# Redistributing the retrieval rows over the attention units of a hybrid streaming encoder step

## The chip, the cores and the metric

The kernel runs on one core of one Trainium2 chip. The metric is the device time in microseconds (us) of one execution. Beside timed runs there is one profiled execution, whose trace gives start and length of every instruction.

Five things work in parallel on a core: TensorE (PE, matrix products; its loads of the stationary operand are listed apart as PEld), VectorE (DVE), ScalarE (ACT), GpSimd (POOL) and the queues that issue transfers (SP's, ACT's, POOL's). Each engine takes its instructions in the order in which the program gives them and meets the others only at semaphores.

## The reference, cut to what matters

One inference step of one encoder layer over 512 prompt tokens and 64 sample tokens, all in fp32:

```python
proj = x @ w_in                                   # q | k | v | u
att  = rms_norm(band_attention(q, k, v, rel_bias))   # 16 heads x 64, chunks of 64, 8 chunks back
ssm  = rms_norm(s5(u))                            # complex diagonal state space, 64 groups
x1   = layer_norm(alpha * x + concat(att, ssm) @ w_out)
# PEER: 8 heads x 16 of 128^2 single-neuron experts per token
a    = einsum('td,tkd->tk', x1, u_tab[idx])       # 128 gathered rows of u per token
y    = einsum('tk,tkd->td', gelu(a) * g, v_tab[idx])
x2   = layer_norm(alpha * x1 + y)
```

The band attention, for one chunk of queries, is `softmax(q k^T / 8 + bias) v` over the visible keys. The PEER part is a product-key retrieval: each token picks 128 experts, whose vectors of 2048 numbers in the tables `u_tab` and `v_tab` have to be fetched from memory.

## The kernel before, in words

**Two groups of tokens.** The first group (64 sample tokens and the first 128 prompt tokens) goes through projections, state space, attention, output projection and the choice of experts first. While the second group (the 384 prompt tokens left) goes through the same steps, VectorE works off the first group's expert rows in the gaps.

**A row.** For a tile of 128 tokens, one *row* is one expert per token: a POOL indirect transfer (L604) gathers 128 vectors of 2048 fp32 numbers, 1 MB, into one of the ring's slots, and one VectorE instruction consumes them. For the table u it is a multiply with a running sum against the tokens in PSUM (L1341), for the table v a multiply-add into PSUM (L1354). In the stage of the change the ring has five slots; `PLACE` says which slot each row takes, and a gather waits until the row that held its slot has been consumed (the semaphore `used`). `rows(n)` on VectorE consumes the next n rows of one fixed list, `ROWS`, wherever it is called.

**The second group's attention.** It has 48 units in eight blocks, one block for each pair of heads: `UNITS_B = [(m, hh, j) for m in range(NPAIR) for j in (1, 2, 3) for hh in range(2)]`. j is the 128-query block, and a unit sees j + 1 chunks of 128 keys. So in each block come two *narrow* units (2 key chunks), two *middle* ones (3) and two *wide* ones (4). For a unit u the engines do this:

- TensorE, `score(u)` (L1633): scores of 128 queries against 256, 384 or 512 keys, into one of two PSUM banks.
- VectorE, `front(u)` (L1158; at a block's first unit L1147 before it): adds the bias into the buffer S[u % 2] and takes the row maximum. It waits for `score(u)` and, since S[u % 2] still holds the unit before last, for **pt_done of unit u - 2**, which is the end of `turn(u - 2)`.
- ScalarE, `exp(u)` (L754).
- VectorE, `back(u)`: reciprocal of the row sums (L1166) and a diagonal matrix of them (L1167), which releases `turn(u)`.
- TensorE, `turn(u)` (L1649): multiplies each key chunk of S[u % 2] by the diagonal, which transposes and normalizes it; ScalarE copies the result out (L771).
- TensorE, `values(u)` (L1675): the product with v.

TensorE's order is `score(u + 2)`, `turn(u)`, `values(u - 1)`, then the next unit. Ahead of a block's first unit comes `v_turn` (L1823), which transposes the block's v, and TensorE waits for ScalarE's copy of it (L938). VectorE's order in one turn of its loop is `front(u + 1)`, one row, `back(u)`, one row. A bias table of 640 KB for each block comes through SP (L393), released by `values` of the last unit of the block before.

Of the kernel before, what the change touches and what calls it, by code (L numbers as in the profile page):

```python
# [129 lines left out]
UNITS = UNITS_A + UNITS_B  # L130
# [21 lines left out]
def build(nc, a, o):  # L152
    ctx = ExitStack()
    with ctx:
# [845 lines left out]
        def _(dve):  # L1000
# [138 lines left out]
            def front(u):  # L1139
                m, hh, j = UNITS[u]  # L1140
                A = u < NUA
                b = m % 2
                Mb = (MbB, MbA)[A][b]
                S, stat = (StB, StA)[A][u % 2], (st, stA)[A][u % 2]
                if u in (0, NUA) or UNITS[u - 1][0] != m:
                    dve.wait_ge(a_in[b], 80 * (m // 2 + 1) if A else 80 * 4 + 16 * (m // 2 + 1))
                    link(nc.vector.memset(Mb[0:CH, :, P - CH:P] if A else Mb[0:CH, :, BW - CH:BW], NEG))  # L1147
                dve.wait_ge(sc_done, u + 1)
                if u >= 2:
                    dve.wait_ge(pt_done, u - 1)  # L1150
                if j < 0:
                    rows, keys, bias = P, T, MbS[b]
                elif j == 0:
                    rows, keys, bias = P, P, Mb[:, hh, :]
                else:
                    rows, keys, bias = P, P * (j + 1), Mb[:, hh, TP - P * j:BW]
                src = acc[0:rows, 1024 * (u % 2):1024 * (u % 2) + keys] if A else L[u % 2][:, 0:keys]
                nc.vector.tensor_tensor_reduce(S[0:rows, 0:keys], src, bias, -1.0, HIGHEST, ALU.add, ALU.min,  # L1158
                                               accum_out=stat[0:rows, 0:1]).then_inc(mn_ready, 1)

            def back(u):
                A = u < NUA
                rows = P
                stat, dg = (st, stA)[A][u % 2], (dgB, dgA)[A][u % 2]
                dve.wait_ge(ex_done, u + 1)
                link(nc.vector.reciprocal(stat[0:rows, 2:3], stat[0:rows, 1:2]))  # L1166
                ts_(dg[0:rows, 0:rows], ident[0:rows, 0:rows], stat[0:rows, 2:3], None, ALU.mult).then_inc(p_ready, 1)  # L1167
# [126 lines left out]
            def gate(t):  # L1294
                rv = rowg[t].rearrange("p (h k) -> p h k", h=PH)
                dve.wait_ge(ge, t + 1)
                link(nc.vector.reduce_sum(hs8, rv, AX.X))
                link(nc.vector.reciprocal(hs8, hs8))
                link(tt(wts[:, t * KK:(t + 1) * KK].rearrange("p (h k) -> p h k", h=PH), rv,
                        hs8.unsqueeze(2).to_broadcast([P, PH, TOPK]), ALU.mult))  # L1300
                if STEPS[t] < KK:
                    link(nc.vector.tensor_copy(wts[TS:P, t * KK:t * KK + STEPS[t]],
                                               wts[TS:P, t * KK + STEPS[t]:(t + 1) * KK]))
                link.zero()
# [69 lines left out]
            def rows(n=1):  # L1374
                for _ in range(n):
                    at_row[0] += 1
                    one_row(next(order))
# [78 lines left out]
            for v in range(NUB):  # L1456
                u = NUA + v
                if v + 1 < NUB:
                    front(u + 1)
                rows()  # L1460
                back(u)
                rows()
                if v == 8:
                    gate(0)
                if v == 16:
                    gate(1)
# [468 lines left out]
```

## Time and profile before

| | |
|---|---|
| timed runs | 3854.83 us median of 3 (3846.39 to 3856.22) |
| profiled execution | 3838.52 us, span of the trace 3836.7 us |
| TensorE clock granted, mean of the span | 0.813 of full speed |
| PE / DVE / ACT / POOL busy | 65% / 72% / 9% / 32% of the span |
| DMA | 1332 MB, mean 347 GB/s |

Times within the trace count from the span's start. The second group's attention runs from about 1228 to 1493 us. A busy time counts only instructions that compute; what an engine spends at a semaphore is idle time. In the lists, a bracket such as `[0.74 <-PE low L1649]` is the idle time just before an instruction and what ended it. Matmul counts are doubled against the program's matrix products: each fp32 product stands as two instructions.

### The profile page before, as it was taken

What the parts mean: (1) busy time and instruction counts of PE and PEld (TensorE: products, weight loads), DVE (VectorE), ACT (ScalarE), POOL (GpSimd) and SP (SyncE); (2) the same over time, 40 slices, a digit from 0 to 9 for tenths busy, and PEclk for the clock granted to TensorE, in tenths of its full rate; (3) what the DMA queues carried; (4) which work ended last, traced back from release to release, by engine and by line L of the source; (5) the groups of instructions that cost most, each with busy time, mean ns of one, the idle gap of its engine ahead of it and who ended that gap; (6) DMA issues with size and microseconds to landing.
All of it is one profiled execution on the core that took longest, in us unless ns stands there. A gap on an engine that the chain in (4) does not pass through costs nothing.

```text
span 3836.7 us, 30525 instructions
## 1 busy us (share of the span) xinstructions
PE 2492.9 (65%) x11272; PEld 1904.8 (50%) x11272; DVE 2769.2 (72%) x3222; ACT 344.9 (9%) x807; POOL 1218.7 (32%) x1290
## 2 busy tenths in 40 slices
PE   6899599987985777978988999999968000000000
PEld 5688487744652444545577877777757000000000
DVE  4330201588989998688789799986553989999998
ACT  0111301100002221001010000000000000000000
POOL 1520000022222332222222222232221367777762
PEclk8899799998997666988999999999989555555555
DMA  7574264599998999999999999999997899999997
GB/s 234 188 225 126 72 219 164 197 341 372 349 359 334 393 411 381 421 383 378 422 396 422 423 424 423 424 423 423 423 379 306 348 340 403 409 410 405 408 411 324
DMA packets 292724, 1332.43 MB, mean 347 GB/s; under 512 B 70176, under 2 KB 132160, under 8 KB 141152
## 3 DMA queue, kind: packets, MB, share of 16 engines
q0 software_dynamic: 140432, 952.56, 61.5%
q1 hardware_dynamic: 119984, 364.49, 25.5%
q10 hardware_dynamic: 32160, 13.43, 1.7%
q8 instruction: 90, 1.47, 0.2%
q14 instruction: 58, 0.48, 0.0%
HBM read 1282.60 MB, written 57.20 MB: 349 GB/s over the span
## 4 chain that ended last, share of the span: by engine, by line
PE 34%; DMA 32%; DVE 18%; POOL 6%; issue 6%; ACTq 1%; ACT 1%; another core or an unknown queue 1%; SPq 0%; DVEq 0%; POOLq 0%
PE low L1526 17%; DMA arena<-in_ut 16%; DMA arena<-in_peer_v,arena 11%; PE low L1869 10%; DVE arena L1341 5%; DVE acc L1354 5%; POOL arena L613 3%; POOL arena L604 3%; DMA arena<-g_scratch 2%; DMA arena<-in_w 2%; DVE low L1354 1%; ACTq L678 1%; PE low L1599 1%; PE acc L1599 1%; DMA arena<-y_scratch_b 1%
## 5 line engine op out<-in xcount | busy, mean ns | idle before, releaser
L1354 DVE SCALAR_TENSOR_TENSOR acc<-arena,acc 128x2048 f32<-128x2048 f32 x443 | 1042.8, 2354 | 276.2 <-DMA arena<-in_peer_v,arena 247.2
L1526 PE MATMUL low<-arena 128*128 128x192 f32 (+1 forms) x4096 | 1068.4, 420 | 106.8 <-DMA arena<-in_w 69.4
L1869 PE MATMUL low<-arena 128*128 128x256 f32 x4096 | 917.5, 384 | 108.6 <-DMA arena<-in_ut 108.5
L1526 PEld LDWEIGHTS low<-arena 128*128 128x128 f32 x4096 | 739.6, 196 | 384.4 <-DMA arena<-in_w 66.1
L1869 PEld LDWEIGHTS low<-arena 128*128 128x128 f32 x4096 | 775.9, 191 | 250.0 <-DMA arena<-in_ut 133.4
L604 POOL DMA_INDIRECT arena<-in_peer_v,arena x576 | 561.5, 975 | 980.2 <-DVE acc L1354 833.4
L1341 DVE SCALAR_TENSOR_TENSOR arena<-arena,acc 128x2048 f32<-128x2048 f32 x320 | 725.0, 2285 | 119.6 <-DMA arena<-in_peer_u,arena 111.7
L604 POOL DMA_INDIRECT arena<-in_peer_u,arena x320 | 319.2, 998 | 1251.3 <-DVE arena L1341 869.6
L1354 DVE SCALAR_TENSOR_TENSOR low<-arena,low 128x2048 f32<-128x2048 f32 x126 | 296.6, 2354 | 18.9 <-DMA arena<-in_peer_v,arena 15.8
L613 POOL DMA_INDIRECT arena<-expert_scratch,arena x256 | 245.6, 959 | 78.0 <-issue 78.0
L861 ACT COPY arena<-low 128x256 f32<-128x256 f32 x128 | 47.7, 372 | 973.2 <-PE low L1869 973.2
L1649 PE MATMUL low<-arena 128*128 128x128 f32 x320 | 81.4, 412 | 65.0 <-DVE arena L1167 63.7
L1649 PEld LDWEIGHTS low<-arena 128*128 128x128 f32 x320 | 65.3, 292 | 112.5 <-DVE arena L1167 108.0
L663 ACT COPY arena<-low 128x192 f32<-128x192 f32 (+1 forms) x112 | 44.6, 399 | 822.0 <-PE low L1526 788.1
L1223 DVE MAX8 arena<-arena 128x8 f32<-128x128 f32 (+1 forms) x120 | 40.5, 338 | 101.8 <-ACT arena L835 98.4
L1074 DVE TENSOR_TENSOR arena<-arena 128x256 f32<-128x256 f32 x32 | 16.9, 528 | 118.0 <-PE acc L1572 117.5
L1158 DVE CUSTOM_DVE_ANT_0 arena<-acc,arena 128x128 f32<-128x128 f32 (+1 forms) x24 | 10.7, 447 | 122.0 <-PE acc L1627 80.5
L1202 DVE SCALAR_TENSOR_TENSOR arena<-arena,acc 128x2048 f32<-128x2048 f32 x2 | 4.6, 2288 | 104.9 <-PE acc L1711 92.9
L1633 PE MATMUL low<-arena 64*128 64x256 f32 (+2 forms) x96 | 66.7, 796 | 13.6 <-DVE arena L1158 9.6
L1675 PE MATMUL low<-arena 128*64 128x128 f32 x320 | 71.8, 382 | 0.0
L853 ACT ACTIVATE arena<-arena 128x16 f32<-128x16 f32 x16 | 3.4, 216 | 690.5 <-DMA arena<-expert_scratch,arena 690.5
L571 POOL TENSOR_TENSOR arena<-arena 128x288 f32<-128x288 f32 x32 | 21.9, 686 | 125.3 <-DMA c_scratch<-arena 99.9
(277 smaller groups left out, 1717.5 us busy)
## 6 DMA issues: line engine op xcount, KB each, us to landing
arena<-in_w SPq DMA_DIRECT2D x128, 1024.0 KB, 7.5
arena<-in_ut SPq DMA_DIRECT2D x128, 1024.0 KB, 23.7
expert_scratch<-arena SPq DMA_DIRECT2D x128, 128.0 KB, 26.0
arena<-in_peer_v,arena POOLq DMA_INDIRECT x576, 12.3
arena<-toeplitz_scratch SPq DMA_DIRECT2D x64, 128.0 KB, 4.5
arena<-c_scratch SPq DMA_DIRECT2D x64, 128.0 KB, 5.3
bias_scratch<-distance_scratch POOLq DMA_DIRECT2D x1, 5120.0 KB, 32.0
x_scratch<-arena ACTq DMA_DIRECT2D x5, 1024.0 KB, 4.2
```

The lines of the kernel that those rows point to most:

```text
L604: pool.indirect_dma_start(out=slot[j], out_offset=None, in_=a["peer_" + kind], in_offset=bass.IndirectOffsetOnAxis(ap=idx[:, t * KK + s:t ...
L613: pool.indirect_dma_start(out=dots[:, 3 * KK + e:3 * KK + e + 1], out_offset=None, in_=ascr, in_offset=bass.IndirectOffsetOnAxis(ap=idxe[: ...
L663: nc.scalar.copy(dst, src).then_inc(slab_out, 1)
L861: nc.scalar.copy(astg[j % 4], L[j % 4][:, 0:NSD]).then_inc(a_out, 1)
L1341: stt(slot[j], slot[j], 1.0, acc[:, :], ALU.mult, ALU.mult, accum_out=dots[:, t * KK + s:t * KK + s + 1]).then_inc(used, 1)
L1354: stt(held, slot[j], wv_, held, ALU.mult, ALU.add).then_inc(used, 1)
L1526: ins = mm(L[n % 2][:, 0:width], wring[n % 2][:, k, :], rhs(k), start=k == 0, stop=k == KT - 1)
L1599: ins = mm(d, CAy[g % 8][hf(g2), r, :], Hs[hf(g2), r, g, 0:width], start=False, stop=r == 1)
L1633: ins = mm(L[u % 2][:, 0:n], qB[hf(hh), m, P * (j - 1):P * j], kT[hf(hh), m, TS:TS + n], start=True, stop=True)
L1649: ins = mm(L[2][:, P * k:P * k + P], S[:, P * k:P * k + P], dg, start=True, stop=True)
L1675: ins = mm(d, vs, PT[:, P * k:P * k + P], start=k == 0, stop=k == j)
L1869: ins = mm(L[j % 4][:, 0:NSD], ud[j % 4][:, k, :], lane(catB, k)[:, P:NB], start=k == 0, stop=k == KT - 1)
```

## The change

In the loop over the 48 units the number of rows at the two places depends on how many key chunks unit u has. A narrow unit has one row ahead of `back(u)` and none behind it, a middle unit one and one as before, a wide unit two ahead and one behind. Two narrow, two middle and two wide units take 12 rows, as six units with two rows each did; the stage consumes 96 rows in either kernel.

```diff
                 u = NUA + v
                 if v + 1 < NUB:
                     front(u + 1)
-                rows()
+                rows((1, 1, 2)[UNITS[u][2] - 1])
                 back(u)
-                rows()
+                rows((0, 1, 1)[UNITS[u][2] - 1])
                 if v == 8:
                     gate(0)
```

Only VectorE's order changes. Two places show it.

VectorE, the second narrow unit of the second block. L1158 is `front` (the width says of which unit; its second row reads the minimum out), L1166 and L1167 are `back`, L1341 is a row of experts. Before:

```order
L1158 ISA arena<-low,arena 128x256
L1158 ISA arena 128x1
L1341 SCALAR_TENSOR_TENSOR arena<-arena,acc 128x2048
L1166 RECIPROCAL arena<-arena 128x1
L1167 TENSOR_SCALAR arena<-arena 128x128
L1341 SCALAR_TENSOR_TENSOR arena<-arena,acc 128x2048
L1158 ISA arena<-low,arena 128x384
L1158 ISA arena 128x1
```

In the changed kernel, the same place:

```order
L1158 ISA arena<-low,arena 128x256
L1158 ISA arena 128x1
L1341 SCALAR_TENSOR_TENSOR arena<-arena,acc 128x2048
L1166 RECIPROCAL arena<-arena 128x1
L1167 TENSOR_SCALAR arena<-arena 128x128
L1158 ISA arena<-low,arena 128x384
L1158 ISA arena 128x1
```

The row between the narrow unit's `back` and the next `front` is gone: L1167 and the 384 wide L1158 now stand next to each other.

VectorE, the first wide unit of the first block, from the `front` of the wide unit behind it to the next block's first `front`. Before:

```order
L1158 ISA arena<-low,arena 128x512
L1158 ISA arena 128x1
L1341 SCALAR_TENSOR_TENSOR arena<-arena,acc 128x2048
L1166 RECIPROCAL arena<-arena 128x1
L1167 TENSOR_SCALAR arena<-arena 128x128
L1341 SCALAR_TENSOR_TENSOR arena<-arena,acc 128x2048
L1147 MEMSET arena 64x2x64
L1158 ISA arena<-low,arena 128x256
```

In the changed kernel:

```order
L1158 ISA arena<-low,arena 128x512
L1158 ISA arena 128x1
L1341 SCALAR_TENSOR_TENSOR arena<-arena,acc 128x2048 x2
L1166 RECIPROCAL arena<-arena 128x1
L1167 TENSOR_SCALAR arena<-arena 128x128
L1341 SCALAR_TENSOR_TENSOR arena<-arena,acc 128x2048
L1147 MEMSET arena 64x2x64
L1158 ISA arena<-low,arena 128x256
```

The wide unit has a second row ahead of its `back`; the one behind it stays.

## Rows read from the trace of the kernel before

**Rows 1.** The page: span, busy time of each engine.

```profile
span 3836.7 us, 30525 instructions
PE 2492.9 (65%) x11272; PEld 1904.8 (50%) x11272; DVE 2769.2 (72%) x3222; ACT 344.9 (9%) x807; POOL 1218.7 (32%) x1290
```

**Rows 2.** Busy time by stretch: stretch, its length, engines, granted clock, DMA share, GB/s.

```profile
1228.10:1492.80 264.70, 196.18 (x665) 125.60 (x665) 257.85 (x384) 64.77 (x161) 89.14 (x96) 0.61 0.99 396
...
1500.00:1515.00 15.00, 7.02 (x16) 3.05 (x16) 9.24 (x11) 4.29 (x7) 0.95 (x1) 0.71 0.55 212
1515.00:1600.00 85.00, 76.47 (x230) 44.63 (x229) 58.64 (x25) 3.35 (x7) 23.41 (x25) 0.95 1.01 422
```

**Rows 3.** Waits of VectorE in the stage: in all, times, longest.

```profile
DVE arena L1341 <- DMA arena<-in_peer_u,arena: 2.4, 2, 2.2
DVE arena L1158 <- PE low L1649: 0.7, 1, 0.7
```

**Rows 4.** Timeline, third block, first narrow unit: start, length, engine.

```profile
1299.45 0.29 DVE L1167 TENSOR_SCALAR arena<-arena 128x128 f32<-128x128 f32 x1
1299.65 2.28 DVE L1341 SCALAR_TENSOR_TENSOR arena<-arena,acc 128x2048 f32<-128x2048 f32 x1
1300.28 0.71 PE L1649 MATMUL low<-arena 128*128 128x128 f32 x4
1300.92 1.09 PE L1675 MATMUL low<-arena 128*64 128x128 f32 x8
1301.86 0.55 DVE L1158 CUSTOM_DVE_ANT_0 arena<-low,arena 128x384 f32<-128x384 f32 x1
1301.94 0.91 PE L1633 MATMUL low<-arena 64*128 64x384 f32 x2
```

**Rows 5.** Timeline, third block, second narrow unit.

```profile
1304.74 0.29 DVE L1167 TENSOR_SCALAR arena<-arena 128x128 f32<-128x128 f32 x1
...
1305.08 1.23 PE L1649 MATMUL low<-arena 128*128 128x128 f32 x4 [2.23 <-DVE arena L1167]
```

**Rows 6.** Timeline, first narrow unit of the first block.

```profile
1231.17 0.29 DVE L1167 TENSOR_SCALAR arena<-arena 128x128 f32<-128x128 f32 x1
1231.56 1.19 PE L1649 MATMUL low<-arena 128*128 128x128 f32 x4 [1.35 <-issue]
```

**Rows 7.** Timeline, first narrow unit of the last block, from the `turn` before it.

```profile
1459.71 2.07 PE L1649 MATMUL low<-arena 128*128 128x128 f32 x8 [0.98 <-DVE arena L1167]
1461.71 1.97 PE L1675 MATMUL low<-arena 128*64 128x128 f32 x8
...
1463.61 0.90 PE L1823 MATMUL low<-arena 128*128 128x128 f32 x3
1464.73 0.29 DVE L1167 TENSOR_SCALAR arena<-arena 128x128 f32<-128x128 f32 x1
1465.09 1.64 PE L1633 MATMUL low<-arena 64*128 64x384 f32 x2 [0.57 <-ACT arena L938]
1466.66 1.22 PE L1649 MATMUL low<-arena 128*128 128x128 f32 x4
...
1468.02 0.56 DVE L1158 CUSTOM_DVE_ANT_0 arena<-low,arena 128x384 f32<-128x384 f32 x1 [0.74 <-PE low L1649]
1469.71 1.65 PE L1633 MATMUL low<-arena 64*128 64x384 f32 x2
```

**Rows 8.** Timeline, second narrow unit of the second block; `turn` at the short length.

```profile
1269.06 0.71 PE L1649 MATMUL low<-arena 128*128 128x128 f32 x4 [1.14 <-DVE arena L1167]
```

**Rows 9.** DMA issues in 1300 to 1400 us: count, KB, median us to landing.

```profile
arena<-bias_scratch SPq DMA_DIRECT2D x3, 640.0 KB, 10.6
arena<-in_peer_u,arena POOLq DMA_INDIRECT x38, 7.9
```

## The prediction

> **What bounds the kernel now.** I first read the page for each engine's share of the span: VectorE leads with 72%, TensorE follows with 65% [rows 1]. A mean over the span says nothing of this change, so next I read the busy times of the stretch in which it acts, 1228.1 to 1492.8 us. There VectorE is busy 257.85 of 264.70 us, TensorE 196.18, and the granted TensorE clock is 0.61 in the mean, so between its two levels of 1.2 and 2.4 GHz it goes back and forth [rows 2]. VectorE bounds the stage: it is idle for 264.70 - 257.85 = 6.85 us in all. Third, the list of its waits: only 2.4 us of them end with a gathered row and 0.7 us with TensorE [rows 3]. Fourth, the timeline of single units, for what lies between `back(u)` and the next `front`.
>
> DMA is close behind: it moves 396 GB/s in the stage against 422 in the stretch after it [rows 2]. The stage's 96 rows of 1.05 MB and eight bias tables of 0.66 MB are 106 MB, which at 422 GB/s take 251 us, 14 us less than the stage has.
>
> **The change part by part.** *VectorE's work.* The same 96 rows, 48 `front` and 48 `back` are there before and after, each with the same shape. So the sum of busy time is unchanged, and what can change is the idle time alone. All there is to gain is the 6.85 us of idle time, 0.18% of the span.
>
> *The row taken from behind the narrow units' `back` (16 of them).* It was cover. After `back(u)` releases `turn(u)`, the next thing VectorE has to do besides a row is `front(u + 2)`, which writes the buffer that `turn(u)` still reads and so waits for its end. Before, the row lies in between. In the third block L1167 starts at 1299.45, the row at 1299.65, `turn` runs from 1300.28 to 1300.99, and `front` follows the row at 1301.86: the wait is hidden [rows 4]. With no row, `front` would be free to start at 1299.65 but has to sit until the `turn` is done. How long it takes from the end of a `turn` to the `front` that waits for it is seen once, in the last block: 1466.66 + 1.22 = 1467.88, and `front` starts at 1468.02, 0.14 us later [rows 7]. So the new wait is (end of `turn`) + 0.14 - (start of L1167 + 0.20).
>
> *First narrow unit of each block.* Up to its `back` nothing has moved within the block (the wide unit before it keeps the row behind its `back`), so the wait can be read off the trace as it stands. In the first block it is 1231.56 + 1.19 + 0.14 - 1231.37 = 1.52 us [rows 6], in the third 1300.99 + 0.14 - 1299.65 = 1.48 [rows 4], in the last 1467.88 + 0.14 - 1464.93 = 3.09, since TensorE comes late there: `turn` and `values` of the wide units, `v_turn`, ScalarE's copy and a `score` stand in its queue first, all at the slow clock [rows 7]. The eight blocks in order give 1.52, 1.25, 1.48, 1.29, 1.13, 1.50, 1.49 and 3.09, together 12.75 us. Of the last, 0.74 is waited already [rows 3, 7], which leaves 12.0.
>
> *Second narrow unit.* Here TensorE finds `p_ready` at once or has to finish `values` and `score` first. After the first `front` come 0.48 us of it, a row of 2.20 and the reciprocal's 0.20, as 1301.86 to 1304.74 shows: 2.88 us to L1167, and 0.34 more to the `turn` [rows 4, 5]. With `turn` at 1.22, the next `turn` may start 1.22 + 0.14 + 2.88 + 0.34 = 4.58 us after the first one did. TensorE is ready 1469.71 + 1.65 - 1466.66 = 4.70 us after it where all ran slow [rows 7] and 1301.94 + 0.91 - 1300.28 = 2.57 where all ran fast [rows 4]; so it is late by 0.12 us at most. The wait is then 0.34 + length of `turn` + 0.14 - 0.20: 1.51 us with a `turn` of 1.23 [rows 5], 0.99 with 0.71 [rows 8]. In the trace five of these eight `turn`s are long and three short. I take the same mix: 5 x 1.51 + 3 x 0.99 = 10.5 us. The bounds are 8 x 0.99 = 7.9 and 8 x (1.51 + 0.12) = 13.0.
>
> *The row added ahead of the wide units' `back`.* It costs what it cost elsewhere, since it is one of the 96. It delays `turn` of the wide unit by 2.2 us, behind which stand `values` and the next `score`; VectorE meets their results only after further rows. It covers no wait that rows 3 names as long. I take nothing, and bound the gain by the 6.85 us of idle time.
>
> *The middle units* keep their order: nothing.
>
> *The gathers.* Three rows follow in a wide unit, at about 2.6 us a row, against 1.05 MB at 422 GB/s = 2.49 us. In the narrow units fewer rows are asked for and the five slots fill; a gather lands 7.9 us after its issue [rows 9], and at 2.6 us a row a slot is wanted again after four others, some 10 us. I take no new wait. The old ones, 2.4 us [rows 3], may vanish, since VectorE falls behind by more than that before; both ends are open, and I take half, -1.2. The bias table is asked for in the narrow units, where DMA has now most room.
>
> *What comes after.* At the stage's end the same three rows follow the last `back`, so the tail up to 1515 us, in which DMA falls to 212 GB/s [rows 2], is as before. All later work hangs on the attention's end through the program order of TensorE and VectorE. The rows there already wait for DMA (VectorE is busy 58.64 of 85 us [rows 2]), and more than five cannot be ahead. The delay passes through in full.
>
> The sum is 12.0 + 10.5 - 1.2 = 21.3 us, say +21. The profiled execution took 3838.52 us, so it would take 3860. It lies 16 us (0.42%) under the median of the timed runs and below the fastest of them, so one run can't serve as the base; I add the difference to the median: 3855 + 21 = **3876 us**. With the mildest terms it is 8 x 1.13 + 7.9 - 0.7 - 2.4 = +14.
>
> **The rivals.** *A. The slow clock spreads.* The block's boundary is covered least where TensorE runs slow, 3.09 us in the last block against 1.13 to 1.52 in the others. Three rows in the wide units leave TensorE idle for 2.2 us more ahead of each wide `turn`. If every boundary then looks like the last, the sum is 8 x 3.09 - 0.74 + 13.0 = +37 us, 3892. For it: the granted clock of the stage is only 0.61 [rows 2]. Against it: `turn` to `score` stand back to back at the boundary, and in the third block that stretch went fast within it [rows 4]. The Trainium skill ("TensorE: Matmul & The Clock Gate", HAM oscillation) says that gaps put the engine back to the slow clock and each burst then starts cold. By that rule each wide `turn` starts slow and this rival gains; the trace agrees in part, since the stage's clock goes back and forth, with 0.71 and 1.23 us for the same four instructions [rows 5, 8].
>
> *B. DMA sets the pace (no change).* If the rows' landing, not VectorE's time, held the stage, waits in the narrow units would use time in which no further row was there, and the wide units would take back what was lost. For it: 396 of 422 GB/s. Against it: VectorE waited for a gather only 2.4 us of 264.7, and at 251 us of transfer the stage can't be under what it is now. In this case the sum is 0 to +5, 3857. It decides only if gather waits already exceed the new ones, which rows 3 denies.
>
> *C. Not slower: the wide units' third row is cover that was lacking.* The mechanism is the late TensorE at the block's end (`turn` of 2.07, `values` of 1.97 [rows 7]): if the added row lets `values` and `score` of the middle units drain ahead, TensorE reaches the boundary early, the narrow `turn`s run at once and the idle 6.85 us go. The price is at most -6.9, giving 3848. It would decide only if `turn` of a narrow unit ended within 0.2 us of its release, and the shortest one takes 0.71 [rows 8].
>
> **How the numbers follow.** The forecast (16 waits of about 1 to 1.5 us, one or two of 3) has a chance of 0.64, A 0.18, B 0.14, C 0.04. A measurement of this kernel can tell 0.3%, 11.6 us, from no change. The forecast and A lie above that even at their mild ends, +14, apart from scatter between runs; I leave them 0.02 of no change: slower 0.80, the same 0.17, faster 0.03. Forecast and A reach from +14 to +37, and the timed runs spread by 10 us. The range takes in most of A and the upper part of B: 3856 to 3894. The forecast's own range is 3866 to 3886.
>
> **What would show it.** In the changed kernel's profile the list of VectorE's waits should have L1158 waiting for L1649 some 16 times, 20 us or more in all, with VectorE's busy time in the stage within 1 us of 257.85 and the stage about 286 us long. The gather waits in the stage should stay at or under 2.4 us. The waits of a block's first narrow unit near 3 us in most blocks, with `turn`s of 1.2 us, would speak for A. A stage of 265 us or less, or gather waits of 10 us and more in the wide units, would prove the reading wrong; so would a stage 21 us longer with an unchanged end.

## The result and the profile after

The changed kernel takes 3880.53 us (median of 14 runs, 3872.0 to 3888.7), the kernel before 3856.01 (14 runs). The ratio is 1.0061 with a 95% interval of 1.005 to 1.0072, so the change costs 23.5 us (19 to 28). Forecast were +21 us and 3876.

The page after, against [rows 1]: VectorE's busy time is the same to 0.7 us (2769.2 before), the span is longer.

```profile
span 3878.7 us, 30525 instructions
PE 2504.8 (65%) x11272; PEld 1913.6 (49%) x11272; DVE 2769.9 (71%) x3222; ACT 344.4 (9%) x807; POOL 1245.3 (32%) x1290
```

Where the time went is best seen between two events that both kernels have: the attention's first L1147 and the L1469 that ends its tail. Busy times by stretch (columns as in [rows 2]), of the kernel before:

```profile
1227.88:1505.32 277.44, 206.48 (x705) 131.80 (x705) 265.00 (x388) 71.76 (x173) 92.77 (x99) 0.62 0.98 394
```

and of the changed one:

```profile
1227.79:1532.99 305.20, 216.41 (x705) 139.32 (x705) 266.61 (x387) 71.37 (x173) 92.76 (x99) 0.59 0.93 359
```

The stretch is 27.8 us longer. VectorE is idle 38.6 us of it instead of 12.4, and DMA falls from 394 to 359 GB/s. The waits of VectorE in the changed kernel name the cause; they answer to [rows 3], and the waits for gathers that stood there are gone. The second line, the wait for the last norm, was there before with 5.3 us:

```profile
DVE arena L1158 <- PE low L1649: 28.8, 16, 3.1
DVE arena L1469 <- ACT arena L962: 5.5, 1, 5.5
```

Sixteen waits of `front` for `turn`, one for each narrow unit, as many as rows were taken from behind a `back`. The timeline of the fourth block's boundary (start, length, engine; only the lines that matter) answers to [rows 7]:

```profile
1328.85 2.08 PE L1649 MATMUL low<-arena 128*128 128x128 f32 x8 [3.36 <-DVE arena L1167]
...
1337.91 2.08 PE L1649 MATMUL low<-arena 128*128 128x128 f32 x8 [4.62 <-DVE arena L1167]
...
1339.92 1.97 PE L1675 MATMUL low<-arena 128*64 128x128 f32 x8
...
1341.82 0.90 PE L1823 MATMUL low<-arena 128*128 128x128 f32 x3
...
1342.89 0.29 DVE L1167 TENSOR_SCALAR arena<-arena 128x128 f32<-128x128 f32 x1
...
1343.29 1.64 PE L1633 MATMUL low<-arena 64*128 64x384 f32 x2 [0.57 <-ACT arena L938]
1344.86 1.22 PE L1649 MATMUL low<-arena 128*128 128x128 f32 x4
...
1346.23 0.56 DVE L1158 CUSTOM_DVE_ANT_0 arena<-low,arena 128x384 f32<-128x384 f32 x1 [3.06 <-PE low L1649]
...
1349.49 1.22 PE L1649 MATMUL low<-arena 128*128 128x128 f32 x4
...
1350.86 0.56 DVE L1158 CUSTOM_DVE_ANT_0 arena<-low,arena 128x384 f32<-128x384 f32 x1 [1.46 <-PE low L1649]
```

The first two PE lines are the `turn`s of the two wide units: TensorE had been idle 3.36 us ahead of one and 4.62 ahead of the other. In the kernel before it had been idle 1.15 and 2.29 us ahead of the same two, and only the first of them ran slow:

```profile
1321.21 2.08 PE L1649 MATMUL low<-arena 128*128 128x128 f32 x8 [1.15 <-DVE arena L1167]
...
1328.07 1.31 PE L1649 MATMUL low<-arena 128*128 128x128 f32 x8 [2.29 <-DVE arena L1167]
```

In the changed kernel all that follows runs at the slow lengths, and VectorE, done with `back` at 1343.18, waits 3.06 us for the first narrow `turn` and 1.46 for the second. The eight first waits are 1.44, 1.21, 3.06, 3.06, 3.06, 1.17, 3.06 and 3.00, together 19.1 us; the eight second ones add up to 9.7.

### The profile page after: what moved, and what is told of

The parts are those of the page before. It is cut to its first block, busy times and chain, and to the rows that moved or that the text cites. A ratio compares the mean times of both kernels' runs of the same rounds, so it can differ in the third digit from the quotient of the medians.

```text
span 3878.7 us, 30525 instructions
## 1 busy us (share of the span) xinstructions
PE 2504.8 (65%) x11272; PEld 1913.6 (49%) x11272; DVE 2769.9 (71%) x3222; ACT 344.4 (9%) x807; POOL 1245.3 (32%) x1290
## 4 chain that ended last, share of the span: by engine, by line
PE 37%; DMA 29%; DVE 15%; POOL 10%; issue 6%; ACTq 1%; ACT 1%; another core or an unknown queue 1%; SPq 1%; DVEq 0%; POOLq 0%
PE low L1526 18%; DMA arena<-in_ut 15%; PE low L1869 10%; DMA arena<-in_peer_v,arena 7%; DVE acc L1354 5%; POOL arena L613 5%; POOL arena L604 5%; DVE arena L1341 4%; DMA arena<-in_w 2%; DMA arena<-g_scratch 2%; PE low L1649 1%; ACTq L678 1%; PE low L1599 1%; PE acc L1599 1%; DVE low L1354 1%
## 5 line engine op out<-in xcount | busy, mean ns | idle before, releaser
L604 POOL DMA_INDIRECT arena<-in_peer_v,arena x576 | 575.3, 999 | 968.5 <-DVE acc L1354 814.7
L1341 DVE SCALAR_TENSOR_TENSOR arena<-arena,acc 128x2048 f32<-128x2048 f32 x320 | 723.9, 2284 | 118.2 <-DMA arena<-in_peer_u,arena 110.5
L1354 DVE SCALAR_TENSOR_TENSOR low<-arena,low 128x2048 f32<-128x2048 f32 x126 | 296.6, 2354 | 28.7 <-DMA arena<-in_peer_v,arena 16.4
L613 POOL DMA_INDIRECT arena<-expert_scratch,arena x256 | 257.2, 1005 | 79.0 <-issue 79.0
L1074 DVE TENSOR_TENSOR arena<-arena 128x256 f32<-128x256 f32 x32 | 16.1, 504 | 119.1 <-PE acc L1572 118.7
L1158 DVE CUSTOM_DVE_ANT_0 arena<-acc,arena 128x128 f32<-128x128 f32 (+1 forms) x24 | 10.6, 447 | 122.4 <-PE acc L1627 79.5
L1633 PE MATMUL low<-arena 64*128 64x256 f32 (+2 forms) x96 | 68.7, 818 | 13.6 <-DVE arena L1158 9.6
```

What stands on the lines that cost most here:

```text
L604: pool.indirect_dma_start(out=slot[j], out_offset=None, in_=a["peer_" + kind], in_offset=bass.IndirectOffsetOnAxis(ap=idx[:, t * KK + s:t ...
L613: pool.indirect_dma_start(out=dots[:, 3 * KK + e:3 * KK + e + 1], out_offset=None, in_=ascr, in_offset=bass.IndirectOffsetOnAxis(ap=idxe[: ...
L1341: stt(slot[j], slot[j], 1.0, acc[:, :], ALU.mult, ALU.mult, accum_out=dots[:, t * KK + s:t * KK + s + 1]).then_inc(used, 1)
L1354: stt(held, slot[j], wv_, held, ALU.mult, ALU.add).then_inc(used, 1)
L1633: ins = mm(L[u % 2][:, 0:n], qB[hf(hh), m, P * (j - 1):P * j], kT[hf(hh), m, TS:TS + n], start=True, stop=True)
```

## The experiments

Each was compared with the kernel before on the same chip, whose median was 3839, 3856 or 3859 us by chip. The table has the length of the stretch defined above (277.44 us before), VectorE's waits for TensorE in it, and the ratio of times. The last column is the ratio's distance from one times that median; the plain differences of the medians lie up to 2.7 us beside it (E1 +12.5, E7 +13.0, E6 +24.3). The stretch, the waits and the clock come from one profiled execution of each kernel.

| kernel | stretch, us | waits, us (times) | ratio, 95% interval | us against before |
|---|---|---|---|---|
| the change | 305.20 | 28.8 (16) | 1.0061 (1.005 to 1.0072) | +23.5 |
| E1 third buffer | 285.33 | 9.3 (8) | 1.0026 (1.0012 to 1.0041) | +10.0 |
| E2 before, third buffer | 275.56 | none | 1.0001 (0.9992 to 1.0011) | +0.4 |
| E3 TensorE kept busy | 293.89 | 18.4 (16) | 1.005 (1.0037 to 1.0063) | +19.2 |
| E4 first narrow only | 291.94 | 16.1 (8) | 1.0033 (1.002 to 1.0046) | +12.7 |
| E5 second narrow only | 288.07 | 10.9 (10) | 1.0022 (1.0012 to 1.0033) | +8.5 |
| E6 reversed | 300.65 | 23.9 (14) | 1.0056 (1.004 to 1.0073) | +21.6 |
| E7 row behind | 288.82 | 12.2 (7) | 1.0039 (1.0026 to 1.0052) | +15.1 |
| E9 buffer and busy | 280.53 | 5.1 (7) | 1.0021 (1.0007 to 1.0035) | +8.1 |
| E10 middle too | 338.73 | 57.4 (32) | 1.0145 (1.0121 to 1.0169) | +55.9 |

**E1 and E2, the buffer that makes `front` wait.**

```diff
-StB = [at(XO + 2816 + 512 * j, 512) for j in range(2)]
+StB = [at(o_, 512) for o_ in (XO + 2816, XO + 3328, H6)]   # used as StB[u % 3]
 # front(u), second group
-dve.wait_ge(pt_done, u - 1)
+dve.wait_ge(pt_done, u - 2)
 # back(u), ahead of writing the diagonal matrix
+dve.wait_ge(pt_done, u - 1)
```

> The changed kernel with three score buffers S in place of two for the second group, so that front(u + 2) no longer waits for the end of turn(u); the wait that guards the diagonal matrix stands in back(u + 2) instead. Rows are distributed 1, 2, 3 as in the changed kernel. Theory (the missing row was cover for that wait): the 16 waits of L1158 on L1649, 28.8 us in the changed kernel, fall to those where the score itself is late, some 1.8 us at a block's boundary at the slow clock, so under 12 us in all; the time is 17 to 28 us under the changed kernel, 0 to +8 us against the kernel before. Rival (the distribution itself costs, through three rows in a run or a gather that is late): the time stays at +20 to +25 us against before.

> The kernel before with the same third score buffer. Theory: before, the rows cover the wait but for 0.7 us, so the third buffer changes nothing: within 3 us of the kernel before. Rival (VectorE's waits before were hidden in other numbers): 5 us faster or more.

With the changed distribution and the third buffer no `front` waits for a `turn` any more. What is left is another wait, for a late `score` (in these kernels the products' lines are two further on, L1635 for L1633). From VectorE's waits of E1:

```profile
DVE arena L1158 <- PE low L1635: 9.3, 8, 2.0
```

The stretch falls by 19.9 us and the time to +10.0. Expected were 0 to +8, and 17 to 28 us less than the change; it is 13.5 less, so the waits came out as expected and the time did not quite. In the kernel before, the buffer is worth nothing (+0.4 us). So rows in a run of three do not cost what the change costs; most of it is the buffer's release, and the 9.3 us for late `score`s are what is left. One boundary of E1's timeline shows what the 9.3 us are:

```profile
1332.10 2.08 PE L1651 MATMUL low<-arena 128*128 128x128 f32 x8 [5.07 <-DVE arena L1169]
...
1336.91 0.29 DVE L1169 TENSOR_SCALAR arena<-arena 128x128 f32<-128x128 f32 x1
...
1337.26 0.91 PE L1635 MATMUL low<-arena 64*128 64x384 f32 x2 [0.57 <-ACT arena L938]
1338.10 0.71 PE L1651 MATMUL low<-arena 128*128 128x128 f32 x4
1338.20 0.56 DVE L1158 CUSTOM_DVE_ANT_0 arena<-low,arena 128x384 f32<-128x384 f32 x1 [1.00 <-PE low L1635]
```

`front` is free at 1337.20 and starts as soon as the `score` is out; before, a row covered this too. The first line matters for the clock: TensorE had been idle 5.07 us ahead of the wide `turn`, longer than the 4.62 of the changed kernel at the same place, and the `turn` ran slow, but here the clock was back at its fast level by the `score` and the narrow `turn` (0.91 and 0.71 us, not 1.64 and 1.22).

**E3, the clock.**

```diff
 # turn(u), ahead of the wait for p_ready
+if u >= NUA and j == 3:
+    for _ in range(6):
+        mm(L[3][:, 384:512], ident, ident, start=True, stop=True)
```

> The changed kernel with six idle products of 128x128 (identity by identity into unused PSUM columns) ahead of each wide unit's turn, where TensorE sits idle for 3.4 to 4.6 us. They do no part of the computation. Theory of the clock: the waits of about 3.06 us at five or six block boundaries come from the slow clock after that idle time; kept busy, TensorE reaches the boundary at the fast clock and these waits fall to 1.1 to 1.3, so the 28.8 us fall to 18 to 20 and the time by 8 to 11 us. Rival (the waits at the boundary have a length of their own): no change, or slower by the products where they are late.

The waits fall by 10.4 us to 18.4, at the expected place: the eight first ones are 1.44, 0.91, 0.91, 1.23, 1.39, 1.96, 0.91 and 1.32 (10.1 in all), the second ones 8.3. The stretch is 11.3 us shorter. The granted clock in it rises from 0.59 to 0.73:

```profile
1222.83:1516.72 293.89, 217.63 (x897) 146.19 (x897) 266.09 (x387) 71.38 (x173) 92.81 (x99) 0.73 0.96 373
```

The same boundary as above, in E3's timeline:

```profile
1329.55 1.16 PE L1652 MATMUL low<-arena 128*128 128x128 f32 x8 [3.01 <-DVE arena L1167]
...
1334.70 1.03 PE L1652 MATMUL low<-arena 128*128 128x128 f32 x4 [1.02 <-DVE arena L1167]
...
1335.88 0.56 DVE L1158 CUSTOM_DVE_ANT_0 arena<-low,arena 128x384 f32<-128x384 f32 x1 [1.23 <-PE low L1652]
```

The wide `turn` takes 1.16 us, not 2.08, and TensorE now waits for VectorE ahead of the narrow `turn`. In the changed kernel all sixteen wide `turn`s take 2.07 or 2.08 us; here the second one of every block takes 1.16. By whole executions the kernel is 4 us faster than the change, with intervals that overlap: the 8 to 11 us expected are shown in the stretch, not in the total. The six products also cost TensorE time of their own, so the rise of the mean clock is in part their own running.

**E4 and E5, one narrow unit each.**

```diff
-rows((1, 1, 2)[UNITS[u][2] - 1])
+m, hh, j = UNITS[u]
+rows(2 if (hh, j) == (0, 3) else 1)
 back(u)
-rows((0, 1, 1)[UNITS[u][2] - 1])
+rows(0 if (hh, j) == (0, 1) else 1)      # E4; E5: (1, 1)
```

> Only the first narrow unit of each block has lost the row behind its back; the first wide unit has gained one ahead of its back, all others have one and one. Theory: the waits are additive by unit, and the first ones are the larger part: 12 to 19 us of waits for L1649, and +10 to +18 us against before. Rival (the two narrow units in a row are needed for the loss): under +5 us.

> Only the second narrow unit of each block has lost the row behind its back; the first wide unit has gained one. Theory: waits of 0.9 to 1.5 us, eight of them, 8 to 12 us in all, and +6 to +12 us against before. Rival (a wait costs nothing unless TensorE is late too): 0 to +3 us.

Both came out as the theory had them (E5's ten waits are one of 0.91 to 1.43 at each second narrow unit, 9.2 us in all, and two of 0.85 at first ones, where TensorE was late in spite of the row). 16.1 + 10.9 = 27.0 us of waits against 28.8, and 12.7 + 8.5 = 21.2 us of time against 23.5: the losses add up by unit, to within the scatter. The shares differ a little: the first units wait 16.1 us in E4 against 19.1 in the change.

**E6 and E10, the cover taken from other units.**

```diff
 # E6: rows (2, 1, 1) ahead of back, (1, 1, 0) behind;  E10: (1, 1, 3) and (0, 0, 1)
```

> The distribution turned round: three rows with a narrow unit (two ahead of its back, one behind), two with a middle one, one with a wide one (ahead of its back, none behind). Theory: the wait is the length of the unit's own turn plus 0.28 us, and a wide unit's turn has twice the instructions: 2.4 us each at the slow clock, 1.4 at the fast, so 16 waits of 23 to 38 us in all for L1158 or L1147 on L1649, and +20 to +36 us against before. Rival (only the narrow units lose, because TensorE comes late at the boundary): 16 waits under 12 us and less than +10 us.

> The changed kernel with the row behind the middle units' back taken away as well and given to the wide ones: 1 and 0, 1 and 0, 3 and 1, twelve a block. Theory: a wait is the length of the unit's own turn plus 0.28 us; a middle unit's turn takes 1.65 us at the slow clock and 0.94 at the fast, so 16 more waits of 1.2 to 1.9 us, 20 to 31 us more, 45 to 62 us in all for L1158 on L1649, and +42 to +58 us against before. Rival (a block's waits are bounded by how far TensorE falls behind at its boundary): no more than +30 us.

E6 puts the rows the other way round and is about as slow: 23.9 us in 14 waits of 0.97 to 2.28. Sixteen waits were expected, but the last two wide units have no `front` behind them, so 14 is all there can be. E10 doubles the gaps and more than doubles the waits, 57.4 us in 32. Both the waits and the time are in the range expected. The first three of the four in its third block (the fourth is 1.85 again) are

```profile
1321.56 0.56 DVE L1158 CUSTOM_DVE_ANT_0 arena<-low,arena 128x384 f32<-128x384 f32 x1 [3.05 <-PE low L1649]
...
1326.18 0.56 DVE L1158 CUSTOM_DVE_ANT_0 arena<-low,arena 128x384 f32<-128x384 f32 x1 [1.46 <-PE low L1649]
...
1331.20 0.69 DVE L1158 CUSTOM_DVE_ANT_0 arena<-low,arena 128x512 f32<-128x512 f32 x1 [1.85 <-PE low L1649]
```

The middle units' wait is 1.85, against 1.46 for the narrow one: it grows with the length of the unit's own `turn` (1.65 and 1.22 us). TensorE was idle 5.1 us or more ahead of every wide `turn` here, and still the first narrow `turn` behind it ran at 0.71 us at three of the seven boundaries.

**E7, the same counts with the row on the other side of `back`.**

```diff
 # rows ahead of back (0, 1, 2), behind (1, 1, 1)
```

> The same 1, 2, 3 rows, but the narrow unit's one row stands behind its back instead of ahead of it, so each front has a row before it again: narrow 0 and 1, middle 1 and 1, wide 2 and 1. Theory (what counts is a row between back and front): the second narrow units' waits vanish or nearly so where TensorE is fast, and at the boundary TensorE is late by as much as before, since back comes 2.2 us earlier: 1 to 3 us each for the first, 0 to 1.6 for the second, 8 to 26 us in all. Rival (number of rows in the narrow unit alone decides, because TensorE's own work there is longer than VectorE's): the same +20 to +25 us as the changed kernel.

Seven waits of 1.13 to 3.06 us are left, all at first narrow units (the first block has none); the second ones have vanished. The stretch is 16.4 us shorter than the change's. With the same number of rows in every unit, the row's place decides for the second units. At the boundary it doesn't take the waits away, since TensorE is late by its queue; they fall from 19.1 to 12.2 us. TensorE ran fast more often there: the first narrow `turn` took 0.71 us at six of the seven boundaries, though it had been idle 2.9 us or more ahead of each wide `turn` as well.

**E9, both at once.** The edits of E1 and E3 together.

> The changed kernel with both edits: the third score buffer (front no longer waits for a turn) and six idle products ahead of each wide unit's turn, which do no part of the computation. With the third buffer alone eight waits of 9.3 us for a late score were left. Theory (these come from TensorE being late at the slow clock): kept busy it is on time, the waits fall under 4 us, and the time is within 6 us of the kernel before. Rival (TensorE is late there at either clock): the 9 us stay, and so do the 10 us of time.

5.1 us of waits for `score` are left, over the 4 expected, and the stretch is 3.1 us longer than before. So the buffer's release and the late TensorE together hold nearly all of the 27.8 us. The time, +8.1 us (3 to 14), misses the 6 expected; where the other 5 us are, outside the stretch or scatter, stays open.

**E8 and E11, a try at a faster kernel.** Two of the 55 later rows are moved into the 5.3 us in which VectorE waits for the last norm (`rows(2)` and `rows(55)` become `rows(4)` and `rows(53)` in the kernel before); E11 has the third buffer as well.

> The kernel before with two of the 55 rows that follow the attention moved into the 5 us in which VectorE waits for the last norm (4 rows there in place of 2). Theory: these 5 us are idle on VectorE and partly on DMA, so the time falls by 3 to 5 us, at the edge of what can be measured. Rival (the later rows wait for DMA anyway and the tail is set by TensorE): no change.

> The kernel before with the third score buffer and two of the 55 later rows moved into the wait for the last norm. Theory: the tail rows bring what they brought alone, 5 to 8 us, and the buffer takes away some single waits of 1 to 2.5 us: 6 to 10 us faster than before. Rival (the tail's gain was scatter): within 3 us of before.

E8 has a ratio of 0.9981 (0.9968 to 0.9994), -7.3 us; the medians differ by -4.9, and 3 to 5 were expected. The wait for the norm falls from 5.3 to 0.7 us with two rows in its place:

```profile
DVE arena L1469 <- ACT arena L962: 0.7, 1, 0.7
```

E11 has 0.9992 (0.9975 to 1.0009), -3 us. Its interval includes no change, and the 6 to 10 us expected did not come. The idle time is filled in both (0.7 and 0.6 us of the wait are left); that the kernel gets faster is shown once and not confirmed.

## Why the prediction was right

- **VectorE's work is the same and only idle time can change.** Right. In the stretch its busy time rose by 1.6 us, more than the 1 us allowed, with the same work. L1167 lasts 0.29 us, but the instruction behind it used to start 0.20 after its start; where `front` waits, the two no longer overlap, 16 x 0.09 = 1.4 us. The prediction counted each wait from the start of the row that was gone, so 0.09 of each is busy time in the profile.
- **The missing row was cover for `pt_done`.** Right, and shown by taking the wait away (E1), by halves (E4, E5), by other units (E6, E10) and by the row's place (E7).
- **First narrow units, 12.0 us.** This is the term that was mis-sized: 19.1 us measured, 18.3 without the 0.74 that was waited before. The formula held, but I read the lateness of TensorE off the trace before, in which one boundary of eight ran slow throughout; in the changed kernel five did (3.00 to 3.06 us). The step that failed is "the wait can be read off the trace as it stands": nothing had moved on VectorE within the block, but TensorE's lengths had changed. That is the price that rival A named, in five blocks rather than eight, and E3, which keeps TensorE at work, takes 9 us of it back.
- **Why five boundaries were slow is not settled.** The longer gaps that rival A named are there: 3.1 to 4.9 us ahead of every wide `turn`, against 0.7 to 2.8 and once 4.3 before. With them all sixteen wide `turn`s are slow, against twelve before. But E1 and E7 leave gaps of 2.9 to 5.1 us, with the wide `turn`s as slow but for one of 1.95, and the first narrow `turn` behind them ran at 0.71 us at six of the seven boundaries in each, against two in the change. So the gap alone does not make a slow boundary; what decides whether TensorE is fast again by the narrow `turn`, no run here isolates.
- **The Trainium skill's rule** ("TensorE: Matmul & The Clock Gate", HAM oscillation), that gaps put the engine back to the slow clock, leaned the right way here. This case's traces agree in part. In the changed kernel every wide `turn` behind such a gap was slow, and the granted clock of the stretch fell from 0.62 to 0.59; with the gaps filled it rose to 0.73. E1 speaks against reading more into it, with gaps as long ahead of the wide `turn`s and a clock of 0.69. A change that spreads one engine's work can change the clock at which the old durations were taken.
- **Second narrow units, 10.5 us.** 9.7 measured, 10.4 with the 8 x 0.09 us counted as the prediction counts them. The mix differed: four waits of 1.43 to 1.46, two of 1.02 and 1.06, two of 0.91 and 0.92, for five long and three short.
- **Gathers, -1.2 us.** The 2.4 us of waits for gathers in the stage all went; three rows in a run brought none. Rival B falls: DMA had room, its rate fell to 359 GB/s.
- **Rival C** falls: no gain is seen in the wide units in any kernel, and reversing the distribution costs as much as the change.
- **The delay passes through in full.** L1469 comes 27.7 us later, and 2000 us further on the L1368 at 3487.56 us still comes 27.8 later, at 3515.37. The timed runs differ by 23.5 (19 to 28). The profiled executions differ by 42, the last 14 of them in the last 350 us; single executions of either kernel scatter by 17 to 28 us, so this pair says nothing about that part. In the experiments above, too, the time moved by what the stretch did, to within 5.4 us.
- **Length of the stage.** It was to be about 286 us long; from the first L1158 to the end of the last L1167 it is 292.

So the sum 21.3 against 23.5 is closer than its terms, and that is in part luck: the boundary was 7 us too low (12.75 against 19.1 + 8 x 0.09), the gain from the gathers was 1.2 us too small, and the timed runs differ by 4 us less than the profiled stretch.

## What to carry to other kernels

Ahead of spreading filler work by the size of the units it stands between, ask for each filler which wait it covers: here the row behind `back` hid the release of a double buffer, and every unit needs that one, however little work it has. The extra filler given to the large units covered nothing, and it left TensorE idle longer just ahead of the place where it is latest; all wide `turn`s behind it were slow. A third buffer took away more than half of the loss, but the distribution was 10 us slower than before even with it, so nothing here speaks for the distribution. Durations of TensorE read off a trace are worth checking at both levels of its clock before they enter a sum.

## What the runs showed of the hardware

Six idle fp32 products of 128x128 in a gap of some 4 us raised the mean granted clock of the stretch from 0.59 to 0.73 and shortened the eight-instruction `turn` behind it from 2.08 to 1.16 us in the fourth block. In E1, where VectorE waits less and nothing is added to TensorE, the clock rose as well, to 0.69, and TensorE's busy time for the same 705 instructions fell from 216.41 to 188.07 us. It did not have less idle time, which a faster TensorE adds to: it was idle for 97.3 of 285.3 us in E1 and for 88.8 of 305.2 in the change. E7 is alike, with 0.67, 189.30 us busy and 99.5 idle. Which pattern of work keeps the fast clock longer stays open.
